# Output stage of a two-group encoder layer: another order of weight sums, splits, fetches and bank reads

## The chip, the cores and the metric

The kernel runs on one core of one Trainium2 chip. The metric is the device time of one launch in microseconds (us), and lower is better. A profiled execution also has a span, from its first to its last instruction.

## What is computed

One layer of a hybrid encoder, for 2048 prompt tokens and 64 sample tokens, with a model width of 1024, all in float32. Three gated branches are run from one projection of the input. Cut to what matters here, the end of the layer is:

```python
gts = jax.nn.sigmoid(gates.astype(f32)).reshape(B, L, N_BRANCH, D_MODEL)
merged = gts[:, :, 0] * y_gla + gts[:, :, 1] * y_pool + gts[:, :, 2] * y_gdn
y = merged.astype(x.dtype) @ w_out            # (tokens, 1024) @ (1024, 1024)
x = x + rmsnorm(y, norm_post)
```

## The kernel before

The last phase, `closing_phase`, has two stages. In the **branch stage** six tiles of 352 tokens are each multiplied with eight blocks of the branch projections (`tile`, L2560 to L2562). VectorE multiplies each result in PSUM by its gates (`gated`, L2645), GpSimd adds the three branches (`merge`, L2852 and L2856), and SyncE stores the sum to memory (`store_merged`, L2308).

The **output stage** multiplies the merged tokens by `w_out`. Its 16 prompt tiles of 128 tokens are taken in eight pairs of 256 tokens (PAIRS), and each pair is one Strassen-like product of 2 by 2 blocks: seven block products, named P1, P6, P5, P7, P2, P3, P4 in the order in which TensorE does them (`product`, `blocks`, L2572 to L2576). The block on the left comes from the pair's tokens and the one on the right from `w_out`. To keep float32 precision each operand is split into a high part (a cast on ScalarE: `high`, L2413, for tokens and `b_part`, L2406, for weights) and a low part (a subtraction on VectorE: `a_low`, L2663, and `b_low`, L2659), and each block product is 12 matmuls of 512 columns.

For the weights the sums T1, T2 and T4 (VectorE, L2736, L2741, L2746) and T3 (GpSimd, L2869) are made once, beside the last tile of the branch stage. B11, B21 and B22 are used as they are. The last 128 rows of `w_out` come by a transfer of their own (L2353).

For the tokens of pair i:

- `load_m(i)` (SyncE, L2331) fetches the pair from memory, 1 MB, into one of two buffers `m_raw`.
- `sums(i)` (GpSimd, L2837 to L2842) makes three sums and one difference: L2837 the sum for P5, L2839 the difference for P7 in place, L2840 the sum for P6, L2842 the sum for P3. There is one set of buffers for the sums of pairs 1 to 7.
- `high(i, j)` waits until product j of pair i-1 has been done, since the split parts have one buffer for each j.
- Four banks of PSUM collect the seven products. `taken(i, j)` reads a bank: P1 and P2 on ScalarE (L2421, L2425), P6, P5, P7, P3, P4 on VectorE (L2672, L2677, L2680, L2683). P3 goes to the bank of P5, so TensorE waits for `taken(i, P5)` before P3, and for `taken(i, P7)` before P4.
- `statistics(t)` (ScalarE, L2442), `norm(t)` (VectorE, L2692 to L2708) and `result(t)` (GpSimd, L2848) normalise tile t of 128 tokens and add x. `store(t)` (SyncE, L2340) writes it, and `load_x(t + 2)` (L2336) then fetches the next x into the same buffer.

What sets the order: each engine has one queue and takes its instructions as they are written down in the code, so a waiting instruction holds all behind it. The order on VectorE, ScalarE, GpSimd and SyncE is written by hand. SyncE's queue is at L2365 to L2374; for pair i it is `load_m(i + 2)` (once all low parts of pair i are made), then for each of its two tiles `store(t)`, the wait for that store, and `load_x(t + 2)`. GpSimd's (L2872 to L2881) is, for pair i, `sums(i + 1)`, `result(2 * i)`, `result(2 * i + 1)`. After the eight pairs the 64 sample tokens pass through the same weights in a plain product.

Of the kernel before, what the change touches and what calls it, by code (L numbers as in the profile page):

```python
# [12 lines left out]
KD = DM // P  # L13
# [2150 lines left out]
B_ORDER = (B11, T1, T2, T3, B21, B22, T4)  # L2164
# [3 lines left out]
def closing_phase(nc, d, late, early):  # L2168
# [6 lines left out]
    with ExitStack() as ctx, Held(nc) as held:  # L2175
# [41 lines left out]
        under = {B11: 0, T1: 1, T2: 2, T3: 3, B21: 4, B22: 5, T4: 6}  # L2217
# [41 lines left out]
        t_sums, t3_ready = sem("t_sums"), sem("t3_ready")  # L2259
# [13 lines left out]
        def split_by(q):  # L2273

            return B_ORDER.index(q) + 1

# [10 lines left out]
        SUM_BEFORE = {P6: 3, P5: 1, P7: 2, P3: 4}  # L2287
# [10 lines left out]
        with nc.Block() as block:  # L2298
            @block.sync
            def _(sp):  # L2300
# [55 lines left out]
                sp.wait_ge(b_split, PRODUCTS)  # L2356
                sp.dma_start(gain[:, :], d["norm_post"].to_broadcast([P, DM])).then_inc(gain_landed, 16)
                for q in range(2):
                    sp.wait_ge(merged_stored[q], 16 * 4 * TILES_B)

                sp.wait_ge(a_split, P4)
                load_m(1)
                load_x(0)
                load_x(1)
# [18 lines left out]
            def _(act):  # L2383
# [85 lines left out]
                act.wait_ge(late.first_landed, 16)  # L2469
                act.wait_ge(late.then_landed, 16)  # L2470
                act.wait_ge(y_ready, LAST * KD + 3)
                b_part(B11, b11_raw)
                act.wait_ge(t_sums, 1)
                b_part(T1, t1_raw[:, :, :])
                high(0, P1)
                act.wait_ge(t_sums, 2)
                act.wait_ge(y_ready, LAST * KD + 5)
                b_part(T2, t2_raw[:, :, :])
                high(0, P6)
                act.wait_ge(t3_ready, 1)  # L2480
# [4 lines left out]
                high(0, P5)  # L2485
                high(0, P7)
                b_part(B21, b21_raw)
                taken(0, P1)
                high(0, P2)
                act.wait_ge(y_gated, TILES_B * KD)  # L2490
                for q in range(2):
                    act.wait_ge(merged_stored[q], 16 * 4 * TILES_B)
                high(0, P3)
                act.wait_ge(w_last_landed, 16)
                b_part(B22, b22_raw)
                act.wait_ge(t_sums, 3)
                b_part(T4, t4_raw)
                act.wait_ge(eps_set, 1)
                act.wait_ge(b_split, PRODUCTS)
                high(0, P4)  # L2500
                taken(0, P2)
                for j in (P1, P6, P5, P7, P2, P3):
                    high(1, j)
                statistics(0)
                high(1, P4)
                statistics(1)
                for i in range(1, PAIRS - 1):
                    taken(i, P1)
# [6 lines left out]
                    high(i + 1, P4)  # L2515
                    statistics(2 * i + 1)
# [30 lines left out]
            def _(pe):  # L2547
# [32 lines left out]
                def product(i, j):  # L2580
                    pe.wait_ge(a_split, PRODUCTS * i + j + 1)
                    if i == 0:
                        pe.wait_ge(b_split, split_by(j))
# [40 lines left out]
            def _(dve):  # L2624
# [32 lines left out]
                def b_low(q, raw):  # L2657
                    dve.wait_ge(b_high, split_by(q))
                    tt(b_lo[q][:, :, :], raw, b_hi[q][:, :, :].bitcast(F32), ALU.subtract).then_inc(b_split, 1)  # L2659

                def a_low(i, j):
                    dve.wait_ge(a_high, PRODUCTS * i + j + 1)
# [66 lines left out]
                for m in range(KD):  # L2729
                    gated(LAST, m)  # L2730
                    if m == 2:
                        b_low(B11, b11_raw)
                    elif m == 3:
                        dve.wait_ge(y_ready, LAST * KD + 4)
                        dve.wait_ge(late.then_landed, 16)
                        tt(t1_raw[:, :, :], b12_raw, b11_raw, ALU.subtract).then_inc(t_sums, 1)  # L2736
                    elif m == 4:

                        dve.wait_ge(w_last_landed, 16)
# [287 lines left out]
```

## Time and profile before

| | us |
|---|---|
| median of 3 runs (2518.72 to 2519.96) | 2519.78 |
| the profiled execution's own time | 2518.89 |
| its span | 2517.1 |
| TensorE busy in the span | 2422.5 (96%) |
| VectorE, ScalarE, GpSimd busy | 1168.3, 713.4, 894.9 |
| mean granted TensorE clock, as a share of 2.4 GHz | 0.984 |

Times in rows are microseconds from the start of the span unless they end in ns. PE is TensorE, DVE is VectorE, ACT is ScalarE, POOL is GpSimd and SPq is SyncE's queue of transfers. A row of the order in time gives the start, the duration, the engine, the line of the code, what is written from what, and in brackets the idle time before it with the instruction that ended it. A matmul's duration overlaps with the next one, so the distance between two starts is its pace.

### The profile page before, as it was taken

The page shows a single profiled execution, that of the slowest core. Times are in us where ns is not written, and L with a number is a line of the kernel's source. Part 1 is how long each engine was busy: PE and PEld are TensorE (multiplying, and loading weights), DVE is VectorE, ACT ScalarE, POOL GpSimd, SP SyncE. Part 2 cuts the span into 40 slices and gives each one's busy share as a digit, 9 for nine tenths or more (in the row PEclk, how much of TensorE's full clock was granted, in tenths as well). Part 3 has the DMA queues.
Part 4 walks back from the last instruction along what each step waited for, and adds up shares of the span by engine and source line. Part 5 has one row for each costly group of instructions (what it writes and reads, how often), then busy time and mean ns, then how long its engine had stood idle before and what let it go on. Part 6 is the DMA issues. An engine that isn't in the chain of part 4 may idle for free. (4 is left out here: it accounts for less than half of the span.)

```text
span 2517.1 us, 37952 instructions
## 1 busy us (share of the span) xinstructions
PE 2422.5 (96%) x14719; PEld 2256.8 (90%) x14719; DVE 1168.3 (46%) x1952; ACT 713.4 (28%) x1438; POOL 894.9 (36%) x793
## 2 busy tenths in 40 slices
PE   7999999999999999999999999999999899997888
PEld 7989999999999999988999999899999799996666
DVE  6620111123476662025656666566666432336655
ACT  6211111110155521112332333223332331322332
POOL 1212211211111212225665556555665133335443
PEclk9999999999999999999999999999999999998899
DMA  4213512101111122423234325542223465353342
GB/s 165 74 69 111 215 56 72 43 34 60 43 52 66 63 77 95 117 76 85 83 85 125 99 84 154 159 132 81 83 82 96 168 241 182 135 201 98 112 139 97
DMA packets 192579, 265.00 MB, mean 105 GB/s; under 512 B 16096, under 2 KB 167920, under 8 KB 186992
## 3 DMA queue, kind: packets, MB, share of 16 engines
q1 hardware_dynamic: 192496, 263.86, 32.3%
q8 instruction: 57, 0.93, 0.2%
q14 instruction: 26, 0.21, 0.0%
HBM read 164.54 MB, written 99.29 MB: 105 GB/s over the span
## 5 line engine op out<-in xcount | busy, mean ns | idle before, releaser
L393 PE MATMUL dense<-h,w_hi 128*128 128x416 f32 (+1 forms) x1640 | 590.8, 360 | 0.0
L394 PE MATMUL dense<-h,w_hi 128*128 128x416 f32 (+1 forms) x1640 | 582.4, 355 | 0.0
L395 PE MATMUL dense<-h,w_lo 128*128 128x416 f32 (+1 forms) x1640 | 581.7, 355 | 0.0
L188 POOL TENSOR_TENSOR w_hi<-w_raw,zero 128x1024 fp32r<-128x1024 f32 x77 | 148.8, 1933 | 1090.8 <-PE dense L395 795.1
L1443 PE MATMUL gate_bank<-h,w_hi 128*128 128x352 f32 x1632 | 421.7, 340 | 0.0
L393 PEld LDWEIGHTS dense<-h,w_hi 128*128 128x128 f32 x1640 | 310.1, 189 | 13.4 <-issue 5.7
L394 PEld LDWEIGHTS dense<-h,w_hi 128*128 128x128 f32 x1640 | 308.9, 188 | 11.3 <-issue 4.5
L395 PEld LDWEIGHTS dense<-h,w_lo 128*128 128x128 f32 x1640 | 309.4, 189 | 7.1
L1443 PEld LDWEIGHTS gate_bank<-h,w_hi 128*128 128x128 f32 x1632 | 272.8, 189 | 8.9 <-issue 0.7
L1443 PE MATMUL gate_bank<-h,w_lo 128*128 128x352 f32 x816 | 263.8, 323 | 0.0
L2560 PE MATMUL y<-o_hi,wo_hi 128*128 128x352 f32 x576 | 189.0, 328 | 14.6 <-DVE prod L2645 7.2
L190 POOL TENSOR_TENSOR w_lo<-w_raw,w_hi 128x1024 fp32r<-128x1024 f32 x77 | 188.1, 2442 | 6.1
L2562 PE MATMUL y<-o_hi,wo_lo 128*128 128x352 f32 x576 | 187.2, 325 | 0.0
L2561 PE MATMUL y<-o_lo,wo_hi 128*128 128x352 f32 x576 | 187.1, 325 | 0.0
L1821 POOL TENSOR_TENSOR gla_att<-gla_att,masked 128x256 f32<-128x256 f32 (+1 forms) x118 | 103.6, 878 | 159.1 <-DVE masked L1961 151.2
L1443 PEld LDWEIGHTS gate_bank<-h,w_lo 128*128 128x128 f32 x816 | 153.8, 188 | 0.0
L1709 ACT COPY X<-x_bank 64x256 f32<-64x256 f32 x164 | 60.0, 366 | 276.8 <-PE x_bank L1507 275.9
L2560 PEld LDWEIGHTS y<-o_hi,wo_hi 128*128 128x128 f32 x576 | 109.5, 190 | 16.9 <-issue 13.3
L2852 POOL TENSOR_TENSOR part<-prod 128x352 f32<-128x352 f32 x48 | 58.0, 1208 | 183.7 <-DVE prod L2645 183.7
L2645 DVE TENSOR_TENSOR prod<-y,gate 128x1056 f32<-128x1056 f32 x48 | 60.2, 1254 | 134.6 <-PE y L2562 133.0
L842 DVE SCALAR_TENSOR_TENSOR row_y<-dense,rows_then_inputs 128x416 f32<-128x416 f32 (+1 forms) x40 | 26.3, 658 | 198.3 <-ACT rows_then_inputs L627 198.3
L2561 PEld LDWEIGHTS y<-o_lo,wo_hi 128*128 128x128 f32 x576 | 109.6, 190 | 0.0
(271 smaller groups left out, 4108.4 us busy)
## 6 DMA issues: line engine op xcount, KB each, us to landing
w_raw<-in_w_in SPq DMA_DIRECT2D x77, 512.0 KB, 5.9
rows_then_inputs<-scratch_feat SPq DMA_DIRECT2D x16, 1856.0 KB, 9.4
scratch_feat<-row_y SPq DMA_DIRECT2D x28, 1056.0 KB, 4.9
gate<-scratch_gates SPq DMA_DIRECT2D x11, 2112.0 KB, 8.7
scratch_gates<-gate_row SPq DMA_DIRECT2D x102, 176.0 KB, 1.8
o_raw<-scratch_branch_out SPq DMA_DIRECT2D x6, 2112.0 KB, 13.4
scratch_h_second<-h SPq DMA_DIRECT2D x2, 4224.0 KB, 19.4
h<-scratch_h_second SPq DMA_DIRECT2D x6, 1408.0 KB, 7.7
```

The source lines that it names most:

```text
L188: nc.gpsimd.tensor_tensor(self.hi[:, p], raw, zeros, ALU.add).then_inc(self.high_ready, 1)
L190: nc.gpsimd.tensor_tensor(self.lo[:, p], raw, self.hi[:, p].bitcast(F32), ALU.subtract).then_inc(self.split_ready, 1)
L393: nc.tensor.matmul(out, w_hi[:, p, k], hi.tile(k, t), start=(k == 0), stop=False)
L394: nc.tensor.matmul(out, w_hi[:, p, k], lo.tile(k, t), start=False, stop=False)
L395: mm = nc.tensor.matmul(out, w_lo[:, p, k], hi.tile(k, t), start=False, stop=(k == KD - 1))
L1443: mm = matmul(gate_bank[:, T % 2, 0:TW], w[:, slot(r), k], h[:, k, t * TW:(t + 1) * TW], start=(k == 0 and part == 0), stop=(k == KD - 1 a ...
L1709: last = copy(X[a:a + HALF], x_bank[a:a + HALF, :, a:a + HALF])
L1821: ins = tt(own, own, halves_packed(masked[0:n, :, l, 0:n // 2], s), ALU.add)
L2560: nc.tensor.matmul(out, wo_hi[m][:, k], h, start=(k == 4 * b), stop=False)
L2561: nc.tensor.matmul(out, wo_hi[m][:, k], l, start=False, stop=False)
L2562: mm = nc.tensor.matmul(out, wo_lo[m][:, k], h, start=False, stop=(k == 4 * b + 3))
L2645: nc.vector.tensor_tensor(prod[:, m % 2], y[:, m % 2, :, 0:BT], g, ALU.mult).then_inc(y_gated, 1)
```

## The change

The order of the weights' high and low parts is new and has lists of its own (HIGH_ORDER, LOW_ORDER). T1 and T2 are summed first, T2 in two parts around the arrival of the last rows, and T3 in two halves. The low part of B21 is made on GpSimd. In the first pair P3's tokens are split ahead of P7's and P2's (FIRST_ORDER). The fetch of pair 1 is issued once the low part of P3 of pair 0 is made. In the loop, VectorE reads a bank ahead of the next pair's low part, `norm` moves behind the start of the next pair, and GpSimd does `sums(i + 1)` and then the results of pair i-1 and not of pair i. The diff, with the lines around each edit cut down and the indentation of the engines' code taken in by 8:

```diff
 B11, T2, T1, T3, B21, B22, T4 = range(PRODUCTS)
-B_ORDER = (B11, T1, T2, T3, B21, B22, T4)
+HIGH_ORDER = (T1, T2, B11, T3, B21, B22, T4)
+LOW_ORDER = (T1, B11, T2, T3, B22, T4)
+FIRST_ORDER = (P1, P6, P5, P3, P7, P2, P4)
 PAIRS = CHUNKS // 2
...
 b_at += [(gate1_at, gate1_at + PIECE), (early.slot_at, early.slot_at + PIECE)]
-under = {B11: 0, T1: 1, T2: 2, T3: 3, B21: 4, B22: 5, T4: 6}
+under = {T1: 0, T2: 1, B11: 2, T3: 3, B21: 4, T4: 5, B22: 6}
 b_hi = {q: over(f"b_hi{q}", b_at[n][0], [P, 4, 512], F32R) for q, n in under.items()}
...
 b_high, b_split = sem("b_high"), sem("b_split")
-t_sums, t3_ready = sem("t_sums"), sem("t3_ready")
+b21_split = sem("b21_split")
+t1_ready, t2_ready, t3_ready, t4_ready = sem("t1_ready"), sem("t2_ready"), sem("t3_ready"), sem("t4_ready")
 a_sums, a_high, a_split = sem("a_sums"), sem("a_high"), sem("a_split")
...
 eps_set = sem("post_eps_set")
-def split_by(q):
-    return B_ORDER.index(q) + 1
+def high_by(q):
+    return HIGH_ORDER.index(q) + 1
+def low_by(q):
+    return LOW_ORDER.index(q) + 1
+def part_by(i, j):
+    return PRODUCTS * i + (FIRST_ORDER.index(j) if i == 0 else j) + 1
 def sums_of(i):
...
             P2: raw[:, 4:KD, 0:P], P3: s4[:, :, :], P4: raw[:, 4:KD, P:2 * P]}[j]
-SUM_BEFORE = {P6: 3, P5: 1, P7: 2, P3: 4}
+SUM_BEFORE = {P5: 1, P6: 2, P7: 3, P3: 4}
 def wait_source(eng, i, j):
...
                 load_m(0)
-        sp.wait_ge(b_split, PRODUCTS)
+        sp.wait_ge(a_split, part_by(0, P3))
+        load_m(1)
+        sp.wait_ge(b_split, low_by(T4))
+        sp.wait_ge(b21_split, 1)
         sp.dma_start(gain[:, :], d["norm_post"].to_broadcast([P, DM])).then_inc(gain_landed, 16)
+        load_x(0)
+        load_x(1)
         for q in range(2):
             sp.wait_ge(merged_stored[q], 16 * 4 * TILES_B)
-        sp.wait_ge(a_split, P4)
-        load_m(1)
-        load_x(0)
-        load_x(1)
         for i in range(PAIRS):
...
         use_log_exp_tables(nc)
-        act.wait_ge(late.first_landed, 16)
-        act.wait_ge(late.then_landed, 16)
-        act.wait_ge(y_ready, LAST * KD + 3)
+        act.wait_ge(t1_ready, 1)
+        b_part(T1, t1_raw[:, :, :])
+        act.wait_ge(t2_ready, 2)
+        b_part(T2, t2_raw[:, :, :])
+        act.wait_ge(y_ready, LAST * KD + 5)
         b_part(B11, b11_raw)
-        act.wait_ge(t_sums, 1)
-        b_part(T1, t1_raw[:, :, :])
         high(0, P1)
-        act.wait_ge(t_sums, 2)
-        act.wait_ge(y_ready, LAST * KD + 5)
-        b_part(T2, t2_raw[:, :, :])
         high(0, P6)
-        act.wait_ge(t3_ready, 1)
+        act.wait_ge(t3_ready, 2)
         act.wait_ge(y_ready, LAST * KD + 7)
...
         high(0, P5)
+        act.wait_ge(part_ready, TILES_B * KD - 1)
+        act.wait_ge(merged_ready, TILES_B * KD - 1)
+        high(0, P3)
         high(0, P7)
         b_part(B21, b21_raw)
+        high(0, P2)
         taken(0, P1)
-        high(0, P2)
+        b_part(B22, b22_raw)
         act.wait_ge(y_gated, TILES_B * KD)
+        act.wait_ge(t4_ready, 1)
+        b_part(T4, t4_raw)
+        act.wait_ge(b_split, low_by(B22))
+        act.wait_ge(b21_split, 1)
+        high(0, P4)
+        high(1, P1)
+        high(1, P6)
+        high(1, P5)
+        high(1, P7)
+        act.wait_ge(merged_ready, TILES_B * KD)
         for q in range(2):
             act.wait_ge(merged_stored[q], 16 * 4 * TILES_B)
-        high(0, P3)
-        act.wait_ge(w_last_landed, 16)
-        b_part(B22, b22_raw)
-        act.wait_ge(t_sums, 3)
-        b_part(T4, t4_raw)
+        taken(0, P2)
+        high(1, P2)
+        high(1, P3)
         act.wait_ge(eps_set, 1)
-        act.wait_ge(b_split, PRODUCTS)
-        high(0, P4)
-        taken(0, P2)
-        for j in (P1, P6, P5, P7, P2, P3):
-            high(1, j)
         statistics(0)
-        high(1, P4)
-        statistics(1)
         for i in range(1, PAIRS - 1):
+            high(i, P4)
+            statistics(2 * i - 1)
             taken(i, P1)
...
             statistics(2 * i)
-            high(i + 1, P4)
-            statistics(2 * i + 1)
+        high(PAIRS - 1, P4)
+        statistics(2 * PAIRS - 3)
         i = PAIRS - 1
...
         def product(i, j):
-            pe.wait_ge(a_split, PRODUCTS * i + j + 1)
-            if i == 0:
-                pe.wait_ge(b_split, split_by(j))
+            pe.wait_ge(a_split, part_by(i, j))
+            if i == 0 and j == B21:
+                pe.wait_ge(b21_split, 1)
+            elif i == 0:
+                pe.wait_ge(b_split, low_by(j))
             if j == P1 and i > 0:
...
         def b_low(q, raw):
-            dve.wait_ge(b_high, split_by(q))
+            dve.wait_ge(b_high, high_by(q))
             tt(b_lo[q][:, :, :], raw, b_hi[q][:, :, :].bitcast(F32), ALU.subtract).then_inc(b_split, 1)
         def a_low(i, j):
-            dve.wait_ge(a_high, PRODUCTS * i + j + 1)
+            dve.wait_ge(a_high, part_by(i, j))
             tt(a_lo[j][:, :, :], a_source(i, j), a_hi[j][:, :, :].bitcast(F32),
...
             if m == 2:
+                dve.wait_ge(late.first_landed, 16)
+                dve.wait_ge(late.then_landed, 16)
+                tt(t1_raw[:, :, :], b12_raw, b11_raw, ALU.subtract).then_inc(t1_ready, 1)
+            elif m == 3:
+                dve.wait_ge(t1_ready, 1)
+                tt(t2_raw[:, 0:3], b22_raw[:, 0:3], t1_raw[:, 0:3], ALU.subtract).then_inc(t2_ready, 1)
+                dve.wait_ge(w_last_landed, 16)
+                tt(t2_raw[:, 3], b22_raw[:, 3], t1_raw[:, 3], ALU.subtract).then_inc(t2_ready, 1)
+            elif m == 4:
+                dve.wait_ge(t2_ready, 2)
+                b_low(T1, t1_raw[:, :, :])
                 b_low(B11, b11_raw)
-            elif m == 3:
-                dve.wait_ge(y_ready, LAST * KD + 4)
-                dve.wait_ge(late.then_landed, 16)
-                tt(t1_raw[:, :, :], b12_raw, b11_raw, ALU.subtract).then_inc(t_sums, 1)
-            elif m == 4:
-                dve.wait_ge(w_last_landed, 16)
-                dve.wait_ge(t_sums, 1)
-                tt(t2_raw[:, :, :], b22_raw, t1_raw[:, :, :], ALU.subtract).then_inc(t_sums, 1)
+            elif m == 5:
+                dve.wait_ge(t2_ready, 2)
+                dve.wait_ge(b_split, low_by(B11))
+                tt(t4_raw, b21_raw, t2_raw[:, :, :], ALU.subtract).then_inc(t4_ready, 1)
                 a_low(0, P1)
-            elif m == 5:
-                b_low(T1, t1_raw[:, :, :])
-                dve.wait_ge(t_sums, 2)
-                tt(t4_raw, b21_raw, t2_raw[:, :, :], ALU.subtract).then_inc(t_sums, 1)
             elif m == 6:
+                dve.wait_ge(t4_ready, 1)
                 b_low(T2, t2_raw[:, :, :])
                 a_low(0, P6)
-                b_low(T3, t3_raw)
         a_low(0, P5)
+        a_low(0, P3)
+        b_low(T3, t3_raw)
         a_low(0, P7)
         taken(0, P6)
-        b_low(B21, b21_raw)
+        a_low(0, P2)
+        dve.wait_ge(merged_ready, TILES_B * KD)
         for q in range(2):
             dve.wait_ge(merged_stored[q], 16 * 4 * TILES_B)
+        taken(0, P5)
         nc.vector.memset(eps[:, :], EPS).then_inc(eps_set, 1)
-        taken(0, P5)
-        a_low(0, P2)
-        a_low(0, P3)
+        b_low(B22, b22_raw)
         taken(0, P7)
-        b_low(B22, b22_raw)
         b_low(T4, t4_raw)
         a_low(0, P4)
-        for j in (P1, P6, P5, P7):
+        a_low(1, P1)
+        taken(0, P3)
+        for j in (P6, P5, P7, P2, P3):
             a_low(1, j)
-        taken(0, P3)
-        a_low(1, P2)
-        a_low(1, P3)
         taken(0, P4)
         dve.wait_ge(gain_landed, 16)
-        norm(0)
-        a_low(1, P4)
-        norm(1)
         for i in range(1, PAIRS - 1):
+            norm(2 * i - 2)
+            a_low(i, P4)
+            norm(2 * i - 1)
+            taken(i, P6)
             a_low(i + 1, P1)
-            taken(i, P6)
+            taken(i, P5)
             a_low(i + 1, P6)
-            taken(i, P5)
             a_low(i + 1, P5)
...
             taken(i, P4)
-            norm(2 * i)
-            a_low(i + 1, P4)
-            norm(2 * i + 1)
+        norm(2 * PAIRS - 4)
+        a_low(PAIRS - 1, P4)
+        norm(2 * PAIRS - 3)
         i = PAIRS - 1
...
             pool.wait_ge(a_sums, 4 * i + 1)
+            tt(s2[:, :, :], s1[:, :, :], a11, ALU.subtract).then_inc(a_sums, 1)
             tt(a21, a11, a21, ALU.subtract).then_inc(a_sums, 1)
-            tt(s2[:, :, :], s1[:, :, :], a11, ALU.subtract).then_inc(a_sums, 1)
-            pool.wait_ge(a_sums, 4 * i + 3)
+            pool.wait_ge(a_sums, 4 * i + 2)
             tt(s4[:, :, :], a12, s2[:, :, :], ALU.subtract).then_inc(a_sums, 1)
...
             merge(LAST, m, m % 2)
-            if m == 4:
+            if m == 3:
+                pool.wait_ge(t1_ready, 1)
                 pool.wait_ge(w_last_landed, 16)
-                pool.wait_ge(t_sums, 1)
-                tt(t3_raw, b22_raw, b12_raw, ALU.subtract).then_inc(t3_ready, 1)
+                tt(t3_raw[:, 0:2], b22_raw[:, 0:2], b12_raw[:, 0:2], ALU.subtract).then_inc(t3_ready, 1)
+            elif m == 4:
+                sums(0)
             elif m == 5:
-                sums(0)
+                tt(t3_raw[:, 2:4], b22_raw[:, 2:4], b12_raw[:, 2:4], ALU.subtract).then_inc(t3_ready, 1)
+        pool.wait_ge(b_high, high_by(B21))
+        tt(b_lo[B21][:, :, :], b21_raw, b_hi[B21][:, :, :].bitcast(F32), ALU.subtract).then_inc(b21_split, 1)
         for i in range(PAIRS):
...
                 if i == 0:
-                    pool.wait_ge(b_split, PRODUCTS)
+                    pool.wait_ge(b21_split, 1)
+                    pool.wait_ge(b_split, low_by(B22))
                     for q in range(2):
...
                 sums(i + 1)
-            result(2 * i)
-            result(2 * i + 1)
+            if i > 0:
+                result(2 * i - 2)
+                result(2 * i - 1)
+        result(2 * PAIRS - 2)
+        result(2 * PAIRS - 1)
 def program(nc, d):
```

## Rows read from the trace of the kernel before

**Rows 1.** Busy time in two stretches: PE, PEld, DVE, ACT, POOL, clock, DMA share, GB/s.

```profile
2321.00:2345.00 24.00, 16.98 (x60) 13.24 (x60) 13.68 (x21) 8.02 (x17) 13.70 (x9) 0.78 0.42 153
...
2393.00:2417.00 24.00, 21.34 (x86) 16.78 (x85) 13.72 (x22) 8.30 (x17) 10.46 (x7) 0.93 0.39 131
```

**Rows 2.** TensorE in order of time: matmuls at starts, after idle stretches, at both paces.

```profile
2289.43 0.39 PE L2572 MATMUL y_tok<-b_hi,a_hi 128*128 128x512 f32 x1
...
2292.00 0.40 PE L2576 MATMUL y_tok<-b_hi,a_lo 128*128 128x512 f32 x1
2297.14 0.80 PE L2572 MATMUL y_tok<-b_hi,a_hi 128*128 128x512 f32 x1 [4.75 <-DVE a_lo L2663]
...
2324.60 0.80 PE L2572 MATMUL y_tok<-b_hi,a_hi 128*128 128x512 f32 x1 [6.34 <-DVE a_lo L2663]
...
2348.49 0.77 PE L2572 MATMUL y<-b_hi,a_hi 128*128 128x512 f32 x1 [6.91 <-DVE y_row L2677]
...
2373.72 0.47 PE L2572 MATMUL y<-b_hi,a_hi 128*128 128x512 f32 x1 [2.68 <-DVE y_row L2677]
...
2375.80 0.63 PE L2574 MATMUL y<-b_lo,a_hi 128*128 128x512 f32 x1
2376.23 0.63 PE L2576 MATMUL y<-b_hi,a_lo 128*128 128x512 f32 x1
...
2477.14 0.40 PE L2572 MATMUL y_tok<-b_hi,a_hi 128*128 128x512 f32 x1
```

**Rows 3.** GpSimd and then VectorE in order of time, around 2367 us.

```profile
2367.15 1.31 POOL L2837 TENSOR_TENSOR sum_then<-m_raw 128x512 f32<-128x512 f32 x1
...
2371.16 1.27 POOL L2842 TENSOR_TENSOR sum_then<-m_raw,sum_then 128x512 f32<-128x512 f32 x1
...
2371.80 1.17 DVE L2663 TENSOR_TENSOR a_lo<-sum_then,a_hi 128x512 fp32r<-128x512 f32 x1 [6.28 <-ACT a_hi L2413]
2372.89 0.68 DVE L2677 TENSOR_TENSOR y_row<-y,u 128x512 f32<-128x512 f32 x1
```

**Rows 4.** VectorE and then GpSimd in order of time, around 2285 us.

```profile
2283.42 2.27 DVE L2659 TENSOR_TENSOR b_lo<-t_raw,b_hi 128x2048 fp32r<-128x2048 f32 x1
2285.62 3.03 DVE L2746 TENSOR_TENSOR w_out_raw<-w_out_raw,t_raw 128x2048 f32<-128x2048 f32 x1
...
2283.57 2.93 POOL L2852 TENSOR_TENSOR part<-prod 128x352 f32<-128x352 f32 x1 [1.80 <-DVE prod L2645]
```

**Rows 5.** The start: TensorE's last block, T3, and ScalarE's casts (ns, min/median/max).

```profile
2283.55 0.43 PE L2560 MATMUL y<-o_hi,wo_hi 128*128 128x352 f32 x1 [1.56 <-DVE prod L2645]
...
2275.06 6.72 POOL L2869 TENSOR_TENSOR w_out_raw<-w_out_raw 128x2048 f32<-128x2048 f32 x1 [1.30 <-DMA w_out_raw<-in_w_out]
...
L2406 ACT CAST b_hi<-w_out_raw x5: 1894/1896/1908, 2261.4 to 2308.3; 128x2048 fp32r<-128x2048 f32 x5
...
L2413 ACT CAST a_hi<-m_raw x25: 603/617/624, 2332.4 to 2477.4; 128x512 fp32r<-128x512 f32 x25
```

**Rows 6.** The chain that ended last, at pair 1's fetch: start, duration, what.

```profile
2314.20 8.36 DMA m_raw<-scratch_merged
2322.56 0.02 issue
```

**Rows 7.** SyncE's queue in order of time: pair 2's fetch, and one pair's issues.

```profile
2317.98 0.62 SPq L2331 DMA_DIRECT2D m_raw<-scratch_merged  x1
...
2391.30 0.34 SPq L2340 DMA_DIRECT2D out_y_prompt<-x_again  x1
2394.76 0.33 SPq L2336 DMA_DIRECT2D x_again<-in_x_prompt  x1
2395.13 0.55 SPq L2331 DMA_DIRECT2D m_raw<-scratch_merged  x1
```

**Rows 8.** Transfers into `m_raw`, issue to landing: three up to 2345 us, then from 2330 us.

```profile
DMA to landing us min/median/max: 7.4/8.4/9.9
...
DMA to landing us min/median/max: 4.2/6.6/7.1
```

**Rows 9.** GpSimd in order of time: an addition of x with VectorE idle, and one beside it.

```profile
2499.73 2.41 POOL L2848 TENSOR_TENSOR x_again<-normed,x_again 128x1024 f32<-128x1024 f32 x1 [12.61 <-DVE normed L2708]
...
2383.95 2.73 POOL L2848 TENSOR_TENSOR x_again<-normed,x_again 128x1024 f32<-128x1024 f32 x1 [11.52 <-DVE normed L2708]
```

## The prediction

> **What bounds the kernel now.** I read first the busy times by stretch, then TensorE's idle stretches, then what the releasing instruction stood behind, and last SyncE's queue. TensorE is 96% busy over the span, so only the output stage has room. Inside it the 24 us from 2321 hold 16.98 us of matmuls at a clock of 0.78 and a settled pair 21.34 us at 0.93 [rows 1]. Matmuls start 0.234 us apart at full clock (2.57 us for 11 steps at the start of the stage) and 0.43 us after an idle stretch, the granted clock then being 1.2 of 2.4 GHz [rows 2]. So a product is 2.8 us, a pair of seven 19.6 us. The pairs take far longer. The first starts at 2289.43, the eighth at 2477.14, and the rest is 2517.1 - 2477.14 = 40.0 us [rows 2]. Seven pairs at full pace would be 137.3 us and they take 187.7: 50 us are to be had, at most.
>
> They go at four places [rows 2]: 4.75 us ahead of P6 of pair 0, 6.34 ahead of P1 of pair 1, 6.91 ahead of P3 of pair 1, then 2.68 ahead of P3 of each of the pairs 2 to 6, each with some matmuls at 0.43. In a settled pair (24.05 us) the cause stands in rows 3: GpSimd begins `sums` only at 2367.15, behind two additions of x, VectorE waits 6.28 us for the cast of P6's sum, and the read of P5's bank (2372.89), on which P3 waits, is queued behind that low part.
>
> **A lock.** The low part at 2371.80 lasts 1.17 us against 0.68, ending 0.54 us after GpSimd's sum (2372.43) [rows 3]. T4's sum (3.03 us) waits for GpSimd's 2.93 us addition, which itself had waited for the low part before it [rows 4]. So a VectorE instruction with two SBUF inputs and a GpSimd one exclude each other and take turns. The bank read at 2372.89, one input in PSUM, I take as free of it.
>
> **The start (pair 0): worth nothing.** T1 and T2 move ahead of the gating of blocks 3 and 4. VectorE then stands still for the last rows of `w_out`, with block 4's gating behind it. They landed at 2275.06 at the latest [rows 5], and TensorE needs that gating one block (2289.43 - 2283.55 = 5.9) before it was ready for its last, at 2283.55 - 1.56 - 5.9 = 2276.1, so this is just covered. The gap of 1.56 us before the last block [rows 5] stays: block 5's gating now stands behind two low parts of 2.27 [rows 4] and a GpSimd addition. `sums(0)` comes ahead of a merge. From 2283.2 the turns are sum, T4's sum, sum, P1's low part, difference, T2's low part, sum, P6's low part: 4 x 1.27 + 2 x 2.2 + 2 x 0.6 = 10.7 [rows 3, 4], so P6 starts near 2294, 3 us earlier. But T3's second half moves behind that merge (2 x 0.9, from rows 4 without the wait): with half of T3's length, 2.3, it ends near 2298.2, then come the cast of 1.90, P5's cast of 0.62 [rows 5], a merge's turn of 0.9 and the low part of 0.6, so P5 starts near 2302. Before it followed P6 at slow clock: 2297.14 + 12 x 0.43 = 2302.3 [rows 2]. Nothing is left of the 3 us. P7 gets worse. T3 took 6.72 us, of which some 2.2 were the turn of T2's sum, so 4.5 [rows 5], and B21's low part on GpSimd has that size. VectorE has made P3's low part (1.5 with a turn) and T3's (2.2) by 2305.6; then GpSimd's comes, and P7's low part waits for it to 2310.1. P7 starts near 2310.8; before it followed P5 at about 2305.6. The Trainium skill, "GPSIMD Engine Reference", section "Engine selection", says to keep elementwise work on VectorE, and by that rule the 2.27 us form would let everything from P7 on come about 2 us sooner. I go by the rows and count the full lock. Products then run to 2323 or so, and P1 of pair 1 waits besides for ScalarE's read of P2's bank, now queued behind P7's cast and so behind `sums(1)`. I take 2324, against 2324.60 before. The stall ahead of pair 1 moves but stays as large. Its old cause does go: `load_m(1)` was issued at 2314.20 and took 8.36 us [rows 6], and now goes out near 2303.5.
>
> **Pair 1.** P5's bank is read behind P1's low part, not behind P6's sum, so P3 of pair 1 no longer stands for 6.91 us. Pair 2 starts near 2324 + 19.6 + 1.5 (cold start) = 2345. Before it was 2348.49 + two products of 2.8 + 2 of slow clock = 2356. Eleven us gained.
>
> **The settled pairs: the fetch becomes the bound.** This is the step that decides. Call M(i) the landing of pair i's fetch. GpSimd does `sums(i)` at once and only behind it the two results of pair i-2. SyncE stores the second of these, waits, loads x, and only then comes `load_m(i + 1)`, whose landing starts `sums(i + 1)`. Before, the results behind `sums(i)` were pair i-1's, and the fetch behind them was that of pair i+2: two pairs for one turn of this loop. Now it is one pair for one turn:
>
> - landing to first sum 0.15 (2322.56 to 2322.72; rows 6 give the landing), four sums 5.3 (2367.15 to 2372.43 [rows 3]);
> - two low parts that take their turn between them, 2 x 0.55 = 1.1 [rows 3];
> - two results of 2.4 with VectorE idle, 4.8 [rows 9], and a low part before each, 1.2 with the dispatch (2.73 beside VectorE [rows 9] is on the way there);
> - end of a result to `load_m`: 2391.30 to 2395.13, 3.8 [rows 7];
> - landing of the fetch 6.6 [rows 8].
>
> Sum 0.15 + 5.3 + 1.1 + 4.8 + 1.2 + 3.8 + 6.6 = 23.0 us a pair, over TensorE's 19.6 and only 1 us under today's 24.05. Where nothing takes turns it is 20.6; with a low part between all sums and two full results of 2.73 and the landing of 7.1 it is 25.3.
>
> Its start: `load_m(2)` goes out once P4's low part of pair 0 is made. From 2310.1 VectorE has four instructions of 0.6, B22's low part, a bank, a turn of `sums(1)`, T4's low part, another turn and P4's low part: 2.4 + 2.2 + 0.6 + 0.8 + 2.2 + 1.3 + 0.6, so about 2320.3 (2317.98 before [rows 7]), with gain and x ahead of it, and lands 8.4 to 9.9 later [rows 8], M(2) = 2329.5, bounds 2326 and 2333. M(7) = 2329.5 + 5 x 23.0 = 2444.5. VectorE reads P7's bank 7.7 after a landing (P1's, P6's and P5's low parts stand ahead), P4 starts 0.15 later, takes 2.8 and about 1.5 of slow clock: pair 7 starts at 2444.5 + 12.2 = 2456.7, against 2477.14. TensorE's idle time moves from P3 to P4 of a pair. The last pair, the sample and the tail keep their 40.0 us: span 2496.7. The profiled run lies 1.8 over its span and 0.9 under the median, so 2498.5 by its own time, and I say **2499**, 21 us faster.
>
> Costed at nothing: the bank reads ahead of low parts (they are the means, priced above); `norm` behind the pair's end (two of 2 us each, in a wait for P6 that lasts until 5.8 us into the pair; results of pair i-1 are not due before M + 6.5); ScalarE's reordering (8.3 of 24 us busy [rows 1]).
>
> **Rivals.**
> 1. *TensorE bound.* The turns cost little and the loop is 20.6 or less: pair 7 at 2345 + 5 x 19.6 = 2443, with its tail and 1.8 the time is 2485. For it: no row has VectorE between two sums. Against: the new order puts three low parts exactly there.
> 2. *Late start.* The locks of pair 0 push `load_m(2)` back by 10 us, and each later landing with it: 2509. For it: `load_m(2)` waits for every weight split. Against: 2320.3 already has the 4.5 us lock.
> 3. *Slower.* The same loop, at SyncE's queue: `load_m` behind store and x. With a low part in every gap and a landing of 9.9 [rows 8] instead of 7.1 it is 25.3 + 2.8 = 28.1. From 28.1 on pair 7 starts 5 us later than before; at 29 the time is 2329.5 + 145 + 12.2 + 40.0 + 1.8 = 2528.5. Against it: the 9.9 was for a fetch behind three other transfers.
> 4. *No difference.* The new orders only trade one wait for another: a loop of 27 gives 2518.5.
>
> **Numbers.** A measurement of this kernel tells about 0.2%, 5 us, from no change. Loop between 21 and 25.3: chance 0.63, and its own range is 2489 to 2512. TensorE bound 0.20; late start 0.09; slower 0.04; no difference 0.04. Faster therefore 0.92. The range for 8 in 10 goes from 2484 (rival 1) to 2512, which leaves out the slow third of the late start, rivals 3 and 4 and what is below TensorE's bound.
>
> **What would show it.** P6 of pair 0 near 2294 and P7 near 2310.8, behind a 4.5 us low part on GpSimd at line of `b21_split`. Pair 1's fetch issued near 2303.5 and no idle stretch ahead of its P3. From pair 3 on, TensorE idle by some 3 us ahead of P4, not P3, released by the read of P7's bank; starts of pairs 23 us apart; `sums` starting within 0.2 us of a landing, the results straight behind it, and `load_m` out 3.8 us after the second. If `sums` wait instead for low parts while fetches land early, or pairs are 19.6 apart, the loop is not the bound and rival 1 holds; if starts are 27 or more apart, rival 3 or 4.

## The result, and the profile after

| | before | after |
|---|---|---|
| median, range, runs | 2519.25 us, 2518.27 to 2519.96, 4 | 2504.29 us, 2501.99 to 2506.02, 4 |
| the profiled execution's own time, span | 2518.89, 2517.1 | 2506.02, 2504.2 |
| output stage, from its first product to the end of the span | 227.7 | 214.2 |

The ratio is 0.994 with a 95% interval of 0.9923 to 0.9958: 15 us faster, where 21 were forecast (2499, range 2484 to 2512). The sign and the bound (the loop of the fetch) came out as forecast; the time is 5.3 us longer than forecast.

TensorE in order of time: the first matmul of the stage, matmuls after idle stretches (P6, P5 and P7 of pair 0, P4 of pair 1, P3 of pairs 4 and 6, P4 of pair 6), and first matmuls of pairs 1, 2 and 7. In brackets is the idle time before it and what ended it. L2589 was L2572, and L2696 and L2699 are the reads of P5's and P7's banks.

```profile
2289.96 0.39 PE L2589 MATMUL y_tok<-b_hi,a_hi 128*128 128x512 f32 x1
...
2293.83 0.50 PE L2589 MATMUL y_tok<-b_hi,a_hi 128*128 128x512 f32 x1 [0.91 <-DVE a_lo L2682]
...
2301.32 0.50 PE L2589 MATMUL y<-b_hi,a_hi 128*128 128x512 f32 x1 [4.42 <-DVE a_lo L2682]
...
2309.82 0.80 PE L2589 MATMUL y<-b_hi,a_hi 128*128 128x512 f32 x1 [3.89 <-DVE a_lo L2682]
...
2323.68 0.40 PE L2589 MATMUL y_tok<-b_hi,a_hi 128*128 128x512 f32 x1
...
2341.95 0.47 PE L2589 MATMUL y<-b_hi,a_hi 128*128 128x512 f32 x1 [1.29 <-DVE y_row L2699]
...
2344.76 0.40 PE L2589 MATMUL y_tok<-b_hi,a_hi 128*128 128x512 f32 x1
...
2404.37 0.77 PE L2589 MATMUL y<-b_hi,a_hi 128*128 128x512 f32 x1 [2.65 <-DVE y_row L2696]
...
2455.93 0.77 PE L2589 MATMUL y<-b_hi,a_hi 128*128 128x512 f32 x1 [3.32 <-DVE y_row L2696]
...
2460.53 0.47 PE L2589 MATMUL y<-b_hi,a_hi 128*128 128x512 f32 x1 [0.20 <-DVE y_row L2699]
...
2463.36 0.40 PE L2589 MATMUL y_tok<-b_hi,a_hi 128*128 128x512 f32 x1
```

Against [rows 2]: pair 0 now stalls at three places (0.91, 4.42 and 3.89 us) and not at one of 4.75 (and one of 0.55), there is no stop ahead of pair 1, which had 6.34, and it starts 0.9 us earlier than before. Pair 1 has lost its stop of 6.91 us ahead of P3, and pair 2 starts at 2344.76 against 2356.88. The gain is 12.1 us there, and only 13.8 at pair 7 (2463.36 against 2477.14): from pair 2 on almost nothing is gained.

What took its place stands in the list of waits from 2330 to 2480 (us in total, times, longest):

```profile
POOL sum_then L2858 <- DMA m_raw<-scratch_merged: 73.9, 6, 15.1
...
PE y L2589 <- DVE y_row L2696: 13.1, 5, 5.0
...
PE y L2589 <- DVE y_row L2699: 3.1, 3, 1.6
```

GpSimd's first sum waits for the landing of the fetch in every pair from 2 on (the six of the list). One turn, GpSimd and then SyncE's queue in order of time:

```profile
2377.50 1.29 POOL L2858 TENSOR_TENSOR sum_then<-m_raw 128x512 f32<-128x512 f32 x1 [13.02 <-DMA m_raw<-scratch_merged]
2378.87 1.60 POOL L2860 TENSOR_TENSOR sum_then<-sum_then,m_raw 128x512 f32<-128x512 f32 x1
...
2383.39 5.63 POOL L2869 TENSOR_TENSOR x_again<-normed,x_again 128x1024 f32<-128x1024 f32 x2
2401.79 1.28 POOL L2858 TENSOR_TENSOR sum_then<-m_raw 128x512 f32<-128x512 f32 x1 [12.77 <-DMA m_raw<-scratch_merged]
```

```profile
2386.24 0.35 SPq L2352 DMA_DIRECT2D out_y_prompt<-x_again  x1
2388.89 0.33 SPq L2348 DMA_DIRECT2D x_again<-in_x_prompt  x1
2389.26 0.43 SPq L2352 DMA_DIRECT2D out_y_prompt<-x_again  x1
2394.40 0.33 SPq L2348 DMA_DIRECT2D x_again<-in_x_prompt  x1
2394.78 0.55 SPq L2343 DMA_DIRECT2D m_raw<-scratch_merged  x1
```

The turn: sums until 2383.39, two results until 2389.02, then 5.76 us until the fetch goes out, then 7.0 until the next sum. The second store is out 0.24 us after its result, so the 5.14 us between it and the next x are the wait for that store. Before, this wait was 3.46 [rows 7]. The first sums of pairs 2 to 7 start at 2328.86, 2352.89, 2377.50, 2401.79, 2428.39 and 2453.36: a turn of 24.9 us on the mean.

### The profile page after: what moved, and what is told of

Its sections match the earlier page's. It is cut to its first block and busy times, and to the rows that moved or that the text cites. A ratio compares the mean times of both kernels' runs of the same rounds, so it can differ in the third digit from the quotient of the medians.

```text
span 2504.2 us, 37958 instructions
## 1 busy us (share of the span) xinstructions
PE 2420.2 (97%) x14719; PEld 2255.6 (90%) x14719; DVE 1192.6 (48%) x1952; ACT 714.0 (29%) x1438; POOL 908.9 (36%) x795
```

## Experiments

Is the turn of the fetch the bound, and through which of its terms? Or is it GpSimd's and VectorE's own work (then fetches that come earlier change little)? "Stage" is the time from the stage's first product to the end of the span of the profiled execution. It leaves out what moves in the phases before: the stage starts between 2287.93 and 2292.18 in these kernels.

**1. The fetch ahead of the results of the pair before.** SyncE's stores and x for a pair come one turn later, so that they stand behind `load_m(i + 2)`.

```diff
-for i in range(PAIRS):
+for i in range(PAIRS + 1):
...
-    for t in (2 * i, 2 * i + 1):
+    for t in (2 * i - 2, 2 * i - 1) if i > 0 else ():
```

> The changed kernel with one edit on SyncE: the two stores and fetches of x in each turn of its loop are those of pair i-1, not of pair i, so that load_m(i + 2) no longer stands behind the results of pair i-1. Theory (the fetch loop bounds the changed kernel at 24.9 us a pair): sums start without waiting for a landing, pairs 19.6 to 20.5 us apart, time 2484 to 2491. Rival (VectorE and GpSimd taking turns is the bound, the late landings only follow it): no change, 2502 to 2506.

Measured: 2484.65 us (2482.71 to 2487.1), ratio 0.9863 [0.9847, 0.988], stage 193.1. TensorE, first matmuls of the pairs 5 to 7:

```profile
2406.11 0.40 PE L2589 MATMUL y_tok<-b_hi,a_hi 128*128 128x512 f32 x1
...
2425.71 0.40 PE L2589 MATMUL y_tok<-b_hi,a_hi 128*128 128x512 f32 x1
...
2445.31 0.40 PE L2589 MATMUL y_tok<-b_hi,a_hi 128*128 128x512 f32 x1
```

GpSimd in the same kernel:

```profile
2385.48 1.31 POOL L2858 TENSOR_TENSOR sum_then<-m_raw 128x512 f32<-128x512 f32 x1 [5.93 <-DVE a_lo L2682]
```

The pairs are 19.6 us apart, TensorE's own pace, and the sums wait for the low parts of the pair before and no longer for a transfer. So the loop of the fetch was the bound, and opening it is worth 20 us.

**2. The results in their old place.** In the changed kernel GpSimd's loop is again `sums(i + 1)`, `result(2 * i)`, `result(2 * i + 1)`.

```diff
-    if i > 0:
-        result(2 * i - 2)
-        result(2 * i - 1)
-result(2 * PAIRS - 2)
-result(2 * PAIRS - 1)
+    result(2 * i)
+    result(2 * i + 1)
```

> The changed kernel with GpSimd's loop as before (sums of pair i+1, then the results of pair i). Theory: the fetch has two pairs for one turn again, the bank reads ahead of the low parts stay, so the stage is bound by TensorE or nearly so: pairs 19.6 to 21 us apart, 2484 to 2493, faster than the change itself. Rival (the sums first on GpSimd are what gained the 15 us): 2512 or more.

Measured: 2488.59 us (2486.07 to 2490.47), ratio 0.9878 [0.9861, 0.9894], stage 198.0, pairs 20.15 apart. SyncE's queue:

```profile
2376.46 0.33 SPq L2348 DMA_DIRECT2D x_again<-in_x_prompt  x1
2378.08 0.34 SPq L2352 DMA_DIRECT2D out_y_prompt<-x_again  x1
2381.39 0.33 SPq L2348 DMA_DIRECT2D x_again<-in_x_prompt  x1
2381.76 0.55 SPq L2343 DMA_DIRECT2D m_raw<-scratch_merged  x1
```

So the results' new place costs 16 us in the changed kernel: without it the change would have been worth 31 us and not 15. The queue shows why: the first x goes out while GpSimd is still at the second result, and the fetch leaves 3.7 us after that result's store (2378.08 to 2381.76), and what it fetches is not for the next sums but for those after them. With the old place the fetch of a pair is again two pairs ahead of its sums, and the turn no longer closes over one.

**3. That edit alone, in the kernel before.** The results of a pair come one turn later, as in the change.

```diff
-    result(2 * i)
-    result(2 * i + 1)
+    if i > 0:
+        result(2 * i - 2)
+        result(2 * i - 1)
+result(2 * PAIRS - 2)
+result(2 * PAIRS - 1)
```

> The kernel before with one edit alone: GpSimd does the results of pair i-1 behind the sums of pair i+1. Theory: the fetch loop closes over one pair here too, some 24.9 us against 24.05 in the settled pairs (5 x 0.9 lost), while pair 1 no longer waits 6.9 us for its P3: 2513 to 2524, about no change. Rival (sums first are what gained): 2506 or less.

Measured: 2510.36 us (2507.94 to 2515.7, 10 runs), ratio 0.9967 [0.9958, 0.9977], stage 216.7. I had put it at 2513 to 2524 and it is faster than that: the same edit gains 9 us here and costs 16 in the changed kernel. The first matmul of P3 of pair 1, and the waits from 2345 to 2480 of this kernel:

```profile
2346.59 0.77 PE L2572 MATMUL y<-b_hi,a_hi 128*128 128x512 f32 x1 [6.42 <-DVE y_row L2677]
...
POOL sum_then L2837 <- DMA m_raw<-scratch_merged: 63.1, 5, 13.9
```

The same loop forms, with sums from 2331.82 to 2454.63 in five turns, 24.6 us each. It turns no faster than the kernel before (24.05), but the sums of pair 2 no longer stand behind results, so the row of turns starts earlier (its first sum at 2331.82, against 2342.02 before, behind two results). The stop of 6.42 us ahead of P3 of pair 1 stays (6.91 before). In run 2, which has VectorE's new order, it is gone.

**4. The fetch ahead of x.** Both stores, then `load_m`, and only then the waits for the stores and the two x.

```diff
+sp.wait_ge(a_split, PRODUCTS)
+load_m(2)
 for i in range(PAIRS):
-    if i + 2 <= PAIRS:
...
-        load_m(i + 2, 2 * P if i + 2 < PAIRS else NS_)
+    store(2 * i)
+    store(2 * i + 1)
+    if i + 3 <= PAIRS:
+        sp.wait_ge(a_split, PRODUCTS * (i + 2))
+        load_m(i + 3, 2 * P if i + 3 < PAIRS else NS_)
     for t in (2 * i, 2 * i + 1):
-        store(t)
```

> The changed kernel with SyncE's turn in another order: store, store, load_m, then the two fetches of x. The loop stays closed over one pair, but 5.3 of the 5.8 us between the last result and load_m go, and the landing shares the transfers with x and may take 2 to 3 us longer. Theory: pairs 21 to 23 us apart in place of 24.9, 2488 to 2496. Rival (turns on the shared port are the bound): 2502 to 2506.

Measured: 2487.27 us (2484.39 to 2491.16), ratio 0.9872 [0.9856, 0.9889], stage 200.9, turns of 20.6. The issues from 2330 to 2470, with KB each and the median us to landing:

```profile
out_y_prompt<-x_again SPq DMA_DIRECT2D x14, 512.0 KB, 2.8
x_again<-in_x_prompt SPq DMA_DIRECT2D x14, 512.0 KB, 7.2
m_raw<-scratch_merged SPq DMA_DIRECT2D x5, 1024.0 KB, 7.2
```

GpSimd in the same kernel, where the second result waits for `norm`:

```profile
2372.51 2.85 POOL L2871 TENSOR_TENSOR x_again<-normed,x_again 128x1024 f32<-128x1024 f32 x1
2377.24 2.41 POOL L2871 TENSOR_TENSOR x_again<-normed,x_again 128x1024 f32<-128x1024 f32 x1 [1.87 <-DVE normed L2729]
```

From the end of the second result (2379.65) to the fetch (2380.05) it is 0.4 us instead of 5.76, and the turn falls by 4.3. Most of the rest goes to the 1.87 us for which the second result now waits, the results being due before `norm` is through: the two take 7.1 us and not 5.6. The fetch's median is 0.4 longer (7.2 against 6.8). The sums still wait for the landing in every turn, so this is the same loop, only shorter. Time and turn are a little below what I had expected.

**5. Both stores together.** The same, with `load_m` behind the x as in the changed kernel: store, store, wait, x, wait, x, `load_m`.

```diff
+store(2 * i)
+store(2 * i + 1)
 for t in (2 * i, 2 * i + 1):
-    store(t)
```

> The changed kernel with SyncE's turn as store, store, then wait, x, wait, x, load_m. In the changed kernel the second store is waited for some 5.2 us, with the first x in flight, against 2.65 us for the first. Theory (the fetch of x beside it is what slows the second store, the term that was sized too small): the second store's wait is 3 to 3.6 us, load_m goes out 1 to 1.5 us sooner, its landing takes up to 1 us longer; 2499 to 2503. Rival (any second store so soon takes 5 us): 2503 to 2506 and the same 5.8 us.

Measured: 2494.06 us (2492.18 to 2498.24), ratio 0.9908 [0.9891, 0.9924], stage 202.4, faster than either expectation. SyncE's queue, where a x2 row is two issues, the first at its start and the second at its end:

```profile
2382.76 3.15 SPq L2352 DMA_DIRECT2D out_y_prompt<-x_again  x2
2385.96 2.92 SPq L2348 DMA_DIRECT2D x_again<-in_x_prompt  x2
2388.92 0.55 SPq L2343 DMA_DIRECT2D m_raw<-scratch_merged  x1
```

GpSimd in the same kernel:

```profile
2379.90 5.64 POOL L2870 TENSOR_TENSOR x_again<-normed,x_again 128x1024 f32<-128x1024 f32 x2
```

From the end of the second result (2385.54) to the fetch it is 3.4 us, against 5.76 in the changed kernel, and the turn is 22.7 against 24.9. The only thing moved is the fetch of the first x, from just ahead of the second store to behind it. The term falls by 2.4 us and the turn by 2.2, so this is what the x ahead of the second store costs, and without it the turn is close to the forecast 23.0. It is the order that counts, and not that the two are in flight together: here the first x goes out 0.4 us behind the second store (2385.57, 2385.96), and the wait for that store is 3.0 us (to 2388.55).

**6. VectorE's old order, with the shifted fetch.** Low parts again ahead of the bank reads, on top of run 1.

```diff
-taken(i, P6)
 a_low(i + 1, P1)
-taken(i, P5)
+taken(i, P6)
 a_low(i + 1, P6)
+taken(i, P5)
```

> The kernel of e1_fetch_shifted with VectorE's old order in the loop, the low part of P1 and P6 of the next pair ahead of the reads of P6's and P5's banks. Theory (with the sums made a whole product early, the low part never waits, so the order on VectorE is worth nothing by itself): 2483 to 2487, pairs 19.6 us apart. Rival (bank reads first are what took the 6.9 and 2.7 us waits away): waits ahead of P3 come back, 2495 or more.

Measured: 2486.59 us (2483.78 to 2487.78), ratio 0.9873 [0.9856, 0.9889], stage 193.8; 19.9 a pair, with 1.37 us idle ahead of P3 in pair 1, 0.47 in pair 2 and no wait for that bank after them. Against run 1 that is no difference that the runs can tell. Once the sums are early, the order of bank reads and low parts is worth next to nothing.

**7. B21's low part on VectorE.** On top of run 1, behind `taken(0, P6)`.

```diff
 taken(0, P6)
+dve.wait_ge(b_high, high_by(B21))
+tt(b_lo[B21][:, :, :], b21_raw, b_hi[B21][:, :, :].bitcast(F32), ALU.subtract).then_inc(b21_split, 1)
...
-pool.wait_ge(b_high, high_by(B21))
-tt(b_lo[B21][:, :, :], b21_raw, b_hi[B21][:, :, :].bitcast(F32), ALU.subtract).then_inc(b21_split, 1)
```

> The kernel of e1_fetch_shifted with B21's low part back on VectorE, behind the read of P6's bank of pair 0. Theory (the 4.5 us instruction on GpSimd holds the shared pair and delays P7 and all behind it): P7 of pair 0 starts some 16 us after the stage's first matmul, not 19.9, pair 1 some 4 us earlier, 2479 to 2482. Rival (pair 0 is held by T3 and by the fetch, the lock only fills a wait): 2484 to 2486 as e1.

Measured: 2482.22 us (2478.89 to 2490.38), ratio 0.9866 [0.9842, 0.989], stage 190.4. In the changed kernel, GpSimd and then VectorE:

```profile
2303.30 5.91 POOL L2896 TENSOR_TENSOR b_lo<-w_out_raw,b_hi 128x2048 fp32r<-128x2048 f32 x1 [1.23 <-ACT b_hi L2419]
...
2304.74 5.02 DVE L2682 TENSOR_TENSOR a_lo<-m_raw,a_hi 128x512 fp32r<-128x512 f32 x1
```

In run 7, VectorE:

```profile
2303.99 0.68 DVE L2682 TENSOR_TENSOR a_lo<-m_raw,a_hi 128x512 fp32r<-128x512 f32 x1
...
2305.20 2.27 DVE L2779 TENSOR_TENSOR b_lo<-w_out_raw,b_hi 128x2048 fp32r<-128x2048 f32 x1
```

The low part on GpSimd waits 1.4 us for its turn, takes 4.5, and holds a VectorE instruction of 0.68 for 5.02 (to 2309.76). On VectorE it is 2.27 and P7 of pair 0 does not wait at all. The stage is 2.7 us shorter. The times of the two kernels overlap, and each against the kernel before run beside it they have one ratio (0.9866, run 1 0.9863), so the gain is read from the profile and not shown by the runs.

**8. That edit alone, in the changed kernel.** The fetch is not shifted here.

```diff
+dve.wait_ge(b_high, high_by(B21))
+tt(b_lo[B21][:, :, :], b21_raw, b_hi[B21][:, :, :].bitcast(F32), ALU.subtract).then_inc(b21_split, 1)
...
-pool.wait_ge(b_high, high_by(B21))
-tt(b_lo[B21][:, :, :], b21_raw, b_hi[B21][:, :, :].bitcast(F32), ALU.subtract).then_inc(b21_split, 1)
```

> The changed kernel with only the low part of B21 moved from GpSimd to VectorE. Theory (the fetch loop runs from load_m of pair 2, which goes out when the start is through): pair 1 starts 3 to 4 us earlier, and each later landing of a weight block too, with the spacing of the sums still about 24.9 us; 2500 to 2502. Rival (the loop absorbs a gain of the start, since its first landing is set by the queue's order and not by the start): landings where they are, 2503 to 2506.

Measured: 2501.7 us (2499.79 to 2504.31), ratio 0.9938 [0.9921, 0.9954]. Its last fetched pair, GpSimd:

```profile
2449.09 1.27 POOL L2860 TENSOR_TENSOR sum_then<-m_raw 128x512 f32<-128x512 f32 x1 [13.00 <-DMA m_raw<-scratch_merged]
```

Its stage starts at 2287.93, so this sum starts 161.2 us into it, against 163.4 in the changed kernel (2453.36 - 2289.96); the four sums before it are 1.6 to 2.2 us earlier too. The fetch of pair 2 goes out 3.6 earlier (27.0 and 30.6 us into the stage). So by the profile more than half of a gain at the start is handed on by the loop, as the theory says, though less than its 3 to 4 us. The runs do not tell the two kernels apart: the medians differ by 2.6, and the ratios are 0.9938 and 0.994.

**9, 10. T3 off the path of P5.** P5 of pair 0 waits 4.42 us for T3. Run 9 (on top of run 7) casts P5's tokens ahead of T3 on ScalarE:

```diff
+act.wait_ge(y_ready, TILES_B * KD)
+high(0, P5)
 act.wait_ge(t3_ready, 2)
-act.wait_ge(y_ready, LAST * KD + 7)
...
-act.wait_ge(y_ready, TILES_B * KD)
-high(0, P5)
```

Run 10 (also on top of run 7) makes the second half of T3 ahead of the first sums on GpSimd:

```diff
 elif m == 4:
+    tt(t3_raw[:, 2:4], b22_raw[:, 2:4], b12_raw[:, 2:4], ALU.subtract).then_inc(t3_ready, 1)
     sums(0)
-elif m == 5:
-    tt(t3_raw[:, 2:4], b22_raw[:, 2:4], b12_raw[:, 2:4], ALU.subtract).then_inc(t3_ready, 1)
```

> As e5_b21_on_vector, and on ScalarE the cast of P5's tokens ahead of T3's. Theory (P5 of pair 0 waits 4.4 us because its cast is queued behind T3's second half, which GpSimd ends late): P5 follows P6 at once, P7 some 2 us earlier than in e5, 2477 to 2480. Rival (T3's low part sets P7 anyway and nothing is gained on e5): 2480 to 2482.

> e5 (fetch shifted, B21's low part on VectorE) with the second half of T3 on GpSimd ahead of the first weight sums instead of behind them. Theory (the start is bound by what P5 and P7 wait for, but the half only changes places with the sums): P5 of pair 0 no longer waits about 4.4 us for T3, but the first sums, and the products' merges behind them on GpSimd, come 2.4 to 4.5 us later; P7 of pair 0 within 1.5 us of e5's place against the stage's start, time 2479 to 2483. Rival (the late half of T3 costs its full 4 us, and nothing stands behind the sums): 2479 or less, with pair 1 starting 26 us or less after the stage's start, against 29.85 in e5.

Measured: 2481.43 us (2478.55 to 2483.21), ratio 0.9851 [0.9835, 0.9868], and 2481.07 (2479.95 to 2484.21), 0.9859 [0.9843, 0.9875]. Stages 191.1 and 190.2 against 190.4 in run 7: neither gains. In run 9, TensorE:

```profile
2298.92 0.50 PE L2588 MATMUL y<-b_hi,a_hi 128*128 128x512 f32 x1 [1.65 <-DVE a_lo L2681]
...
2305.74 0.80 PE L2588 MATMUL y<-b_hi,a_hi 128*128 128x512 f32 x1 [3.76 <-DVE a_lo L2681]
```

The 2.8 us saved ahead of P5 are lost ahead of P7, which needs T3's low part too. In run 10 P5's stop falls to 2.45 us, but P6 waits 1.98 instead of 0.90 and P4 2.18 instead of 1.54. Runs 7, 9 and 10 are one result within their intervals, 35 to 37 us below the kernel before (2517.65 and 2517.7 beside them) and 22 to 23 below the changed one. They have the lowest medians of all, but their intervals reach over run 1's too, so what is shown beyond noise is the shift of the fetch.

## Why the prediction was right, and where it was off

**The start: right.** P6 was put near 2294, P5 near 2302, P7 near 2310.8 and pair 1 at 2324; they came at 2293.83, 2301.32, 2309.82 and 2323.68. The last of these is in part luck: P7 came 1 us early, but all its twelve matmuls ran at the slow clock (granted clock 0.50 from 2309.82 to 2315.10, 5.3 us against 2.8), which had been given about 1 us, and no wait of pair 1 for the read of P2's bank shows. The lock on the low part of B21 was priced in full, and run 7 shows what that row meant. The rule of the Trainium skill, "GPSIMD Engine Reference", section "Engine selection", from which a gain of about 2 us would follow, points the right way by the profiles: 2.7 us of the stage with an open loop (run 7), about 2 at each landing with a closed one (run 8). No difference in the times of runs shows either of them.

**Pair 1: right.** No stop ahead of its P3; pair 2 was put at 2345 and starts at 2344.76. The 1.5 us above 19.6 had another cause than forecast: there was no cold start (the granted clock is 1.00 from 2323.68), but P4 waited 1.29 us for P7's bank, so that this term is right by luck.

**The loop: right in kind.** The results straight behind the sums, the fetch behind them and the sums at the landing are all there, and run 1 shows that nothing else held the pairs. `load_m(2)` was put near 2320.3 and went out at 2320.53; M(2) was put at 2329.5 and the sums started at 2328.86.

**The step that failed is "end of a result to `load_m`: 2391.30 to 2395.13, 3.8".** Measured it is 5.8 to 6.2 us in four turns and 8.3 in one, 6.3 on the mean. The row was taken from a kernel in which `norm` separates the two results. SyncE's queue of before, the first tile's x:

```profile
2389.34 0.33 SPq L2336 DMA_DIRECT2D x_again<-in_x_prompt  x1
```

It is out 1.96 us ahead of the second store (2391.30 [rows 7]). The forecast itself put the results back to back, which brings the first x to 0.37 us ahead of that store. I moved the work and kept the price that it had in its old place. Run 5 tests this: with the first x behind the second store the term falls to 3.4 us. The other terms of the turn that begins at 2377.50, in the prediction's order: sums and low parts 5.9 (5.3 + 1.1 forecast), results 5.6 (4.8 + 1.2), issue to sum 7.0 (6.6 + 0.15). They sum to 18.5 where 19.15 was forecast (5.3 + 1.1 + 4.8 + 1.2 + 6.6 + 0.15), so the term that failed is more than the whole of the excess in this turn (24.3 against 23.0).

In the sum: five turns of 24.9 and not 23.0 put the last landing at 2453.2, 8.7 us later than the forecast 2444.5. From there to pair 7 it was 10.2 and not 12.2, and the rest 40.8 and not 40.0. 8.7 - 2.0 + 0.8 = 7.5, the difference of the spans (2504.2 and 2496.7). Some 2 us of it are one wait, the 5.04 us store in the last section, whose cause is open. The medians differ by 5.3 and not 7.5, which is no merit of the forecast: it had put the profiled execution 0.9 us under the median, and it lay 1.7 over it (2506.02, 2504.29).

**"TensorE's idle time moves from P3 to P4": wrong.** The larger stop is still ahead of P3, 13.1 us against 3.1 over the pairs. The read of P5's bank now stands behind P1's low part, and I counted only that it no longer stands behind P6's sum. But P1's tokens come by the same fetch, so P3 waits for the landing all the same, VectorE in order of time:

```profile
2453.96 1.22 DVE L2682 TENSOR_TENSOR a_lo<-m_raw,a_hi 128x512 fp32r<-128x512 f32 x1 [5.87 <-ACT a_hi L2426]
2455.10 0.68 DVE L2696 TENSOR_TENSOR y_row<-y,u 128x512 f32<-128x512 f32 x1
...
2459.70 0.68 DVE L2699 TENSOR_TENSOR y_row<-y,y_row 128x512 f32<-128x512 f32 x1
```

P3 starts 2.7 us after the landing (2455.93), and P4 runs at full pace (2460.53 to 2463.36 is 2.8 us). The 1.5 us of slow clock that I had put behind P4 fell behind P3, where the wait for P7's bank swallowed them. That is most of the 2.0.

**The rivals.** TensorE bound (2485) was not what happened, but it is what run 1 gives with two edited lines, 2484.65. The late start fell with the start's own rows (the fetch of pair 2 at 2320.53). The slower loop had its place right, SyncE's queue, and its price wrong: one turn of 26.6 us was the longest, against the 28.1 from which it would have been slower. No difference wanted turns of 27, and they were 24.9.

## What to carry to other kernels

Follow the issue queue as a loop: if the transfer that feeds the next turn stands behind a store of this turn, the turn is compute plus store plus fetch. Move the fetch ahead of the stores (run 1) or of the wait for the last one (run 4), or take the results off the path between the sums and the fetch (run 2). Faster work elsewhere left the turn as it was (run 8). When work is moved, price its transfers by what will be in flight beside them in the new place, not by the row of the old one. An edit can gain in one kernel (9 us, run 3) and cost in another (the results' new place takes back 16 of the 31 us that the change would have brought without it), so try the parts of a change without each other.

## What the runs showed of the hardware that was not expected

The wait for a 512 KB store depends on when the 512 KB fetch ahead of it in the queue went out. With none it is 2.65 us (2386.24 to 2388.89). With an x issued some 1.63 us ahead (run 2) it is 3.3 to 3.7, with one some 1.95 us ahead (before) 3.1 to 3.5, and with one 0.37 us ahead (after) 5.1 to 5.6. With the x 0.4 us behind the store (run 5, the turn shown) it is 3.0. In run 1 the 1 MB fetch goes out 2.26 us ahead of the first store, and the wait is 4.7 to 6.9. The transfers of the changed kernel from 2386 to 2396, in slices of 0.25 us (busy share of the DMA engines in tenths, then GB/s):

```profile
DMA  0000799993000009954286689999994200000972
GB/s 0 0 0 0 279 426 426 393 426 148 0 0 0 0 0 131 197 131 82 49 229 98 229 295 360 410 426 393 442 426 197 98 0 0 0 0 0 131 131 98
```

The store alone (2387.0 to 2388.5) moves at some 400 GB/s. The x and the store behind it begin with 2 us at 49 to 229 GB/s (2389.75 to 2391.75) and only then reach 400. What holds them there was not tried.

One wait of the changed kernel fits none of this. It belongs to the long turn, SyncE's queue:

```profile
2410.52 0.35 SPq L2352 DMA_DIRECT2D out_y_prompt<-x_again  x1
2415.56 0.33 SPq L2348 DMA_DIRECT2D x_again<-in_x_prompt  x1
2415.93 0.43 SPq L2352 DMA_DIRECT2D out_y_prompt<-x_again  x1
...
2421.56 0.55 SPq L2343 DMA_DIRECT2D m_raw<-scratch_merged  x1
```

The first store takes 5.04 us with nothing of the queue ahead of it. It makes that turn 26.6 us long instead of some 24.5. Nor is it alone: runs 5 and 8 have a first store of 4.4 us each (issued at 2404.45 and 2406.85), where their others take some 2.6. The cause stays open.
